# A decoder step with 32 experts: the gather in another order, and the requests for the experts' second matrices moved from SyncE's queue to ScalarE's

## What is computed

```python
logits = x2d @ router_w + router_b
top_val, top_idx = top_k(logits, 4);  top_w = softmax(top_val)
hgu = xb @ moe_w_gu[e] + moe_b_gu[e]           # (1024) x (1024, 2048), per expert
gate, up = min(hgu[:, :1024], 7), clip(hgu[:, 1024:], -7, 7)
act = (up + 1) * gate * sigmoid(1.702 * gate)
out = act @ moe_w_down[e] + moe_b_down[e]      # (1024) x (1024, 1024)
y[token] += top_w * out;   x = layernorm(alpha * x + y)
```

## Time and profile before

| | us |
|---|---|
| median of 3 runs | 1276.86 (1275.33 to 1278.38) |
| the profiled execution, its own time | 1272.98 |
| its span in the profile | 1271.2 |
| granted TensorE clock, mean | 0.99 |
| TensorE busy (matmul) | 1194.8 (94%) |
| HBM read | 450.30 MB |

### The profile page before, as it was taken

How to read it: one execution, slowest core, us unless ns; L and a number is a source line. 1 busy time by engine, 2 the same in 40 slices (tenths; PEclk the granted TensorE clock), 3 DMA queues, 4 the chain that set the end, 5 groups by cost and what they waited for, 6 DMA issues and landing times.

```text
span 1271.2 us, 17367 instructions
## 1 busy us (share of the span) xinstructions
PE 1194.8 (94%) x6686; PEld 655.9 (52%) x6686; DVE 385.2 (30%) x719; ACT 278.8 (22%) x505; POOL 19.2 (2%) x39
## 2 busy tenths in 40 slices
PE   8999999999999999999999997999999999999995
PEld 8998878994434343434434343344443434343441
DVE  4888577853020202021220202212112020202025
ACT  5685444432111010101011110010111111010101
POOL 1000021000000000000000000000000000000000
PEclk9999999999999999999999997999999999999998
DMA  9746477987899999999999997999999999999992
GB/s 286 221 132 176 156 223 252 346 306 300 334 418 417 417 418 418 418 418 417 418 418 418 418 418 307 399 416 418 418 417 419 418 417 417 417 418 417 417 417 78
DMA packets 118349, 456.90 MB, mean 359 GB/s; under 512 B 10408, under 2 KB 49336, under 8 KB 85312
## 3 DMA queue, kind: packets, MB, share of 16 engines
q1 hardware_dynamic: 115728, 447.08, 88.8%
q0 software_dynamic: 2576, 9.21, 2.3%
HBM read 450.30 MB, written 5.95 MB: 359 GB/s over the span
## 4 chain that ended last, share of the span: by engine, by line
PE 88%; DVE 5%; ACT 3%; issue 3%; DMA 0%; DVEq 0%; SPq 0%; ACTq 0%
PE pool L958 33%; PE pool L881 18%; PE ub L841 10%; PE pool L603 5%; PE pool L604 5%; PE pool L605 5%; PE ob L969 3%; PE ub L969 2%; ACT arena L1204 1%; PE pool L871 1%; PE pool L897 1%; PE ob L909 1%; PE pool L954 1%; ACT wh L1014 1%; DVE wl L1260 1%
## 5 line engine op out<-in xcount | busy, mean ns | idle before, releaser
L958 PE MATMUL pool<-gu_w,arena 128*64 128x512 f32 x1920 | 418.8, 594 | 0.0
L958 PEld LDWEIGHTS pool<-gu_w,arena 128*64 128x64 f32 x1920 | 138.1, 137 | 263.9 <-issue 258.9
L881 PE MATMUL pool<-dn_w,arena 128*64 128x512 f32 x1024 | 226.7, 595 | 20.3 <-ACT arena L1204 20.3
L1680 DVE TENSOR_SCALAR arena<-pool 128x512 f32<-128x512 f32 x31 | 21.4, 692 | 729.4 <-PE pool L958 724.5
L603 PE MATMUL pool<-xh,wh 128*128 128x264 f32 x568 | 164.6, 290 | 4.1 <-ACT wh L1014 1.7
L605 PE MATMUL pool<-xh,wl 128*128 128x264 f32 x568 | 161.4, 284 | 0.0
L881 PEld LDWEIGHTS pool<-dn_w,arena 128*64 128x64 f32 x1024 | 70.8, 137 | 156.0 <-issue 128.5
L841 PE MATMUL ub<-x_in,arena 8*128 8x128 f32 x720 | 127.7, 307 | 0.0
L1199 ACT ACTIVATE arena<-arena 128x512 f32<-128x512 f32 x32 | 20.1, 629 | 454.6 <-DVE arena L1680 454.6
L841 PEld LDWEIGHTS ub<-x_in,arena 8*128 8x128 f32 x720 | 97.6, 187 | 38.7 <-issue 11.5
L603 PEld LDWEIGHTS pool<-xh,wh 128*128 128x128 f32 x568 | 107.7, 190 | 11.2 <-issue 5.9
(11 more groups left out here) (319 smaller groups left out, 791.6 us busy)
## 6 DMA issues: line engine op xcount, KB each, us to landing
gu_w<-in_moe_w_gu SPq DMA_DIRECT2D x252, 1024.0 KB, 15.1
dn_w<-in_moe_w_down SPq DMA_DIRECT2D x256, 512.0 KB, 11.2
dn_w<-in_w_in SPq DMA_DIRECT2D x24, 1024.0 KB, 6.1
dn_w<-in_w_branch SPq DMA_DIRECT2D x8, 1024.0 KB, 5.6
gu_w<-in_state_gla POOLq DMA_DIRECT2D x8, 512.0 KB, 6.8
out_gla_sample<-gu_w POOLq DMA_DIRECT2D x8, 512.0 KB, 5.1
dn_w<-in_w_o SPq DMA_DIRECT2D x4, 1024.0 KB, 9.2
arena<-in_moe_w_gu SPq DMA_DIRECT2D x4, 1024.0 KB, 8.4
```

What stands on the lines that cost most here:

```text
L881: last = mm(DOWN[s * CAP:(s + 1) * CAP, :], act_t[:, k % 4, k // 4 * CAP:(k // 4 + 1) * CAP], dn_w[:, k, s * HF:(s + 1) * HF], start=(k == ...
L958: last = mm(out, xg[:, k, j * CAP:(j + 1) * CAP], gu_w[:, k, cols], start=False, stop=(k == NB - 1))
```

## The change

The second matrices' blocks are no longer requested by SyncE but by ScalarE, all eight at once, behind its own two copies of the second products (`output_rows`). SyncE keeps the first matrices. The gather of all pairs takes the order that `gather_first` had, in two halves with a semaphore count for each, and ScalarE waits for each half on its own. The experts' numbers, sizes, buffers and arithmetic stay, but for the order of the products within a PSUM bank.

```diff
@@ block.sync
                 for k in range(NB):
                     sp.wait_ge(gu_used, n * NB + k + 1 - NB)
                     load_gu(k, e)
-                for k in range(NB):
-                    sp.wait_ge(dn_used, n * NB + k + 1 - NB)
-                    load_dn(k, e)
...
-            for e in (1, 2):
-                for k in range(NB):
-                    sp.wait_ge(dn_used, (e - 1) * NB + k + 1)
-                    load_dn(k, e)
-
             at = moe_loops(sp, body)
@@ block.tensor
-            def gather_first(half):
+            def gather(half, then):
 
                 for t, (first, rows) in ((2, TILES[2]), (0, TILES[0]), (1, TILES[1])):
                     for c in range(4):
                         n = 4 * half + c
                         last = mm(GATH[:, half, c * P:(c + 1) * P], ytok[0:rows, t, n * P:(n + 1) * P], pick[0:rows, t, :],
                                   start=(t == 2 and c == 0), stop=(t == 1), skip_group_check=True)
-                last.then_inc(gath0, 1)
-
-            def gather():
-
-                for n in range(NB):
-                    for t in (2, 0, 1):
-                        rows = TILES[t][1]
-                        last = mm(GATH[:, n // 4, n % 4 * P:(n % 4 + 1) * P], ytok[0:rows, t, n * P:(n + 1) * P],
-                                  pick[0:rows, t, :], start=(t == 2), stop=(t == 1))
-                last.then_inc(gath_done, 1)
+                last.then_inc(then, 1)
...
-                        gather()
+                        for half in range(2):
+                            gather(half, gath_done)
@@ block.scalar
             def gathered(it):
 
-                sc.wait_ge(gath_done, it + 1)
                 for b in range(NB):
+                    if b % 4 == 0:
+                        sc.wait_ge(gath_done, it * 2 + 1 + b // 4)
...
+            def load_dn(e):
+
+                for k in range(NB):
+                    sc.dma_start(dn_w[:, k, :], w_down[0, bass.ds(e, 1), k * P:(k + 1) * P, :]
+                                 .rearrange("e p n -> (e p) n")).then_inc(dn_in[k], 16)
...
                     output_rows(n, j, 1 if final and j == 1 else 2)
+                    if not (final and j == 1):
+                        load_dn(E - 1 if final else 0 if j and pair is PAIRS - 1 else pair * 2 + j + 1)
...
                 if n:
                     output_rows(0, 0)
+                    load_dn(1)
                 turned_act(n)
             gathered(0)
             output_rows(1, 1)
+            load_dn(2)
@@ block.vector
-                            v.wait_ge(gath_done, it)
+                            v.wait_ge(gath_done, it * 2)
```

More of the change, by code:

```diff
@@ L850, in turn_weights @@
                 last.then_inc(done, 1)
-            gather_first(0)
+            gather(0, gath0)
             for name in ("yt11", "yt21", "lg", "rk"):
@@ L892, in first_pair @@
                     if k == 4:
-                        gather_first(1)
+                        gather(1, gath0)
                     pe.wait_ge((xg0_act, xg0_dve)[k // 4], k % 4 + 1)
```

## The result

| | before | after |
|---|---|---|
| median, us | 1276.14 (1275.33 to 1278.38, 4 runs) | 1310.38 (1302.98 to 1314.14, 4 runs) |
| ratio | | 1.0258, 95% interval 1.0214 to 1.0302 |
| profiled execution, own time / span, us | 1272.98 / 1271.2 | 1307.53 / 1305.4 |
| granted TensorE clock, mean | 0.99 | 0.971 |

The change makes the kernel slower by 34 us, 2.6%. The forecast was slower by 72.

A forecast was written before the change was run, and what follows sets the result against it. TensorE was taken to set the pace, 29.57 us per expert, with DMA almost level at 30.2. A loop of 1.22 + 2.2 + 27.9 + 0.89 makes 32.2: 28 x 2.64 - 1.6 = +72 on 1276.86, 1349 us; range 1277 to 1395.

The forecast's parts named there:

- the second matrix gets one third: In the loops, queues take turns by packets, 4.1 KB against 8.2 KB: 139 of 417 GB/s for the second matrix.
- the gather's saving swallowed: In 15 gathers, 2.29 us saved each would not shorten the time, as the second matrix's landing sets the pace.
- half a gather at the price of the first pair: Each half gather takes 3.11 us, as in the first pair; two take 6.22 instead of 8.51 us.
- experts 16 and 31 without a wait: Expert 16 follows the section between the loops, expert 31 has no further first matrix requested: no wait at either.
- 64 to 65: Sign in the loops: a pair of experts takes 64 to 65 us instead of 59.13.
- copies before the request: 1.22 us: Loop term: ScalarE requests the second matrix only when its two copies end, 1.22 us behind the last product.
- 2.36 - 1.22 = 1.1 us alone: Loop term: time the second matrix transfers alone before SyncE's next first-matrix request, moving 0.46 MB.
- in steady state both kinds of expert take 32.2: In both loops, experts with scatter or gather take 32.2 us each, 2.64 more than 29.57, for 28 experts.
- 2.2 + 27.9: Loop terms: 2.2 us from request to landing beyond the transfer, and 27.9 us transfer of the second matrix.
- Half or more for the second matrix: Rival: turns go by bytes, waits fall on first matrices, pace 30.2 us per expert; +5, 1282 us; chance 0.13.
- Served as requested: Rival: requests keep their order across queues, the gather's saving comes through until the DMA pace; -8, 1269 us; chance 0.14.
- The clock did fall: Rival: after waits TensorE's clock halves for the last block's products, 0.89 to 1.77 us; +25, 1374 us; chance 0.08.

The follow-up runs named there:

- late in one queue: Kernel before with the new gather; SyncE requests all eight second-matrix blocks after their last use, ahead of the next first matrix; 1269.73 us, ratio 0.9961.

## Why the prediction was right and wrong

**Right.** The direction and the cause: "the second matrix gets one third" (139 GB/s measured), the wait before the second products released by ScalarE's DMA, the gather's saving swallowed (15 x 2.31 us), half a gather at the price of the first pair, the eighth block after about 28 us in the mean, experts 16 and 31 without a wait (7.09 us and a step of 27.98). The prediction took gathers to pay only where TensorE sets the pace; the gather alone shows 19 of 34.7 us.

**Wrong: the size, +34 instead of +72.** The signs that went with it are missed as well: a pair takes 61.6 us in the mean and not 64 to 65, and the DMA engines move 406 and 399 GB/s in the loops and not 390. The steps that failed:

- "*copies before the request: 1.22 us*". ScalarE's requests go out while its copies still run; the first leaves at most 0.2 us behind the last product in all 28 experts. Putting it behind the copies, 1.2 us later, gives this term its price: 40 us, which is as much as the whole miss (38).
- "*2.36 - 1.22 = 1.1 us alone*", which "*moves 0.46 MB*". SyncE's request follows 2.0 to 2.3 us after ScalarE's, in the eight experts behind a long wait 3.1 to 4.0. Its first packet moves 3.4 to 4.0 us behind it; ScalarE's moves after 1.0 us where the engines are free, and after up to 3.3 us behind open blocks of the first matrix. The sum gave both queues the same start and had no open blocks. When the next first matrix's packets start, 0.8 to 1.4 MB of the second have moved in the experts that wait and 1.5 to 2.5 MB in the others, and not 0.46. At the measured 345 to 395 GB/s alone, a microsecond alone is worth 2.5 to 2.8 of shared time.
- "*in steady state both kinds of expert take 32.2*". There is none. In the 16 experts that wait, the landing is the forecast's: 30.2 us in the mean after the request, where its 2.2 + 27.9 are 30.1. After a long wait SyncE's queue has run empty and the first products take 14.5 to 15.4 us, so the next second matrix is alone for longer, lands within 22.5 to 26.4 us and isn't waited for. Then the first matrix catches up and the wait is back. With the first term alone put right the formula would give 0.2 + 2.2 + 25.8 + 0.9 = 29.1 us, under the DMA engines' 30.2; the measured 30.8 lies above, as long waits leave them idle (share 0.89) and lower the clock. So the errors did not all point one way, and the first alone does not make the forecast right.

**The rivals.** Half or more for the second matrix didn't happen, but when it was made to, the waits did move to the first matrices, as that rival said. "Served as requested" needed one queue: late in one queue is 1270, its 1269. The rule of the Trainium skill beside it ("DMA: Bandwidth & Descriptors", section "Issuing engines are not separate DMA queues"), taken as saying that nothing but issue time changes, is answered by 1270 against 1310 for the same requests at the same point of the program. The clock did fall, in part (at 1044.35 the last four products behind a wait took 1.97 us, at full speed 0.9): 20.7 us more busy time for the same products. Some of it surely counts: the eight experts behind a long wait have no wait for a DMA at all, and still take 1.0 to 1.8 us more than the 28.33 or 28.51 us of TensorE's work at full clock, 11 us together. But the slower products also put SyncE's next request off and so spare waits. What the clock costs in all wasn't separated.

## What to carry to other kernels

In this kernel two queues that both had work shared by packets, not by bytes or by the order of the requests, and the stream with the smaller rows got the smaller part. If one engine needs both streams in turn, keep them in one queue in the order of use: it was the faster way in every pair of runs here. Where a late stream must share, its time alone at the start decides: work out when the rival's first packet moves, not when its request is written, what of the rival is still open at that moment, and how much of the late stream has moved by then. And before a saving on the bounding engine is counted in full, take the pace of the second resource (30.1 us here, against 29.6) and the room in hand: they let through 19 of 35 us.

## What the runs showed of the hardware

- ScalarE's requests didn't wait for its earlier copies to end: the first went out 0.16 us after the start of the first of two 0.58 us copies. Behind a wait for the copies they came 1.2 us later.
- The time from a request to its first packet was not the same in both queues: 3.4 to 4.0 us for SyncE's, made while ScalarE's blocks were under way, and 1.0 us for ScalarE's on free engines. What holds SyncE's back isn't shown.
- Fully busy engines moved 410 GB/s over a whole loop with 4 KiB packets alone and 418 with two in three bytes in 8 KiB packets, 2% that cost this kernel 21 us. For 2 us at 1052, with ScalarE's queue alone, they moved 345 GB/s at a share of 1.00.
- The granted clock was 1.00 in the loops before. About second products that were stretched by waits it was 0.89 (394 to 426) and 0.91 (1045.5 to 1069), and the first products that followed took 15.36 us at 1046.97 instead of 13.90.
